# Layer norms on rows in place, by token halves, with the next stage's first two units going token by token

## The reference, cut to what matters

```python
# first block (one layer)
x = x + merged @ w_out
h = rmsnorm(x, g_mlp)
x = x + square(relu(h @ w_mlp_in)) @ w_mlp_out
h = rmsnorm(x, g_final)

# second block; post_norm(x, sub, g, b) = layer_norm(ALPHA * x + sub, g, b)
for layer in range(2):
    if layer == 1:
        shared = nsa_shared_kv(h, ...)          # six key/value slots, kv_w
    h = post_norm(h, 0.5 * swiglu(h, w1, w3, w2), ln_g[layer, 0], ln_b[layer, 0])
    mix = chunked_sgu_mixer(h, ...) if layer == 0 else nsa_mixer(h, shared, ...)
    h = post_norm(h, mix, ln_g[layer, 1], ln_b[layer, 1])
    h = post_norm(h, 0.5 * swiglu(h, w1, w3, w2), ln_g[layer, 2], ln_b[layer, 2])
return h
```

## Time and profile before

| what | us |
|---|---|
| median of 3 runs | 1635.03 |
| lowest, highest run | 1631.24, 1640.81 |
| span of the profiled execution | 1638.5 |
| TensorE busy in it | 1546.8 |
| VectorE, ScalarE, GpSimd busy | 928.9, 712.0, 152.5 |

### The profile page before, as it was taken

The page is one execution under the profiler, slowest core; times in us unless marked ns, Lnnn a source line. Parts: engine busy times, 40 slices in busy tenths (PEclk is TensorE's granted clock), DMA queues, the critical chain, the costliest instruction groups (busy, mean ns, idle before and its releaser), DMA issues.

```text
span 1638.5 us, 26119 instructions
## 1 busy us (share of the span) xinstructions
PE 1546.8 (94%) x10700; PEld 1395.6 (85%) x10700; DVE 928.9 (57%) x1372; ACT 712.0 (43%) x924; POOL 152.5 (9%) x85
## 2 busy tenths in 40 slices
PE   8878979999999999999999998999999899999997
PEld 6868877998889999898789997999998866689996
DVE  5835266655575555667765557544555373365556
ACT  5436534434344443653344444344433464344442
POOL 0124510000020000200120002000001300110001
PEclk9969999999999999999999999999999987999999
DMA  8853343655666555553455653675554510255561
GB/s 256 138 145 95 117 150 129 205 179 182 197 225 196 196 184 180 181 181 139 144 183 182 189 193 129 183 254 182 191 191 134 181 51 1 77 180 180 182 196 58
DMA packets 191020, 267.75 MB, mean 163 GB/s; under 512 B 5581, under 2 KB 164465, under 8 KB 190687
## 3 DMA queue, kind: packets, MB, share of 16 engines
q1 hardware_dynamic: 186192, 250.05, 47.0%
q0 software_dynamic: 3872, 15.39, 4.0%
q10 hardware_dynamic: 878, 1.21, 0.3%
HBM read 261.40 MB, written 4.19 MB: 162 GB/s over the span
## 4 chain that ended last, share of the span: by engine, by line
PE 85%; DVE 7%; ACT 5%; DMA 2%; issue 1%; SPq 0%; POOL 0%; DVEq 0%; ACTq 0%
PE bank L627 83%; DMA ring<-in_w_in 2%; DVE hT_lo L1633 1%; PE bank L650 1%; ACT act_out L1246 1%; ACT split L1228 1%; DVE split L1554 1%; DVE xn L1605 1%; ACT hT_hi L1254 1%; DVE act_out L1625 0%; DVE stats L1580 0%; DVE xn L1811 0%; ACT attend L1328 0%; ACT arena L1276 0%; DVE attend L1742 0%
## 5 line engine op out<-in xcount | busy, mean ns | idle before, releaser
L627 PE MATMUL bank<-hT_hi,split 128*128 128x256 f32 x4240 | 771.0, 282 | 22.7 <-DVE hT_lo L1633 17.1
L1554 DVE TENSOR_TENSOR split<-ring,split 128x2048 fp32r<-128x2048 f32 x218 | 496.9, 2284 | 440.6 <-ACT split L1228 440.5
L627 PEld LDWEIGHTS bank<-hT_hi,split 128*128 128x128 f32 x4240 | 658.2, 189 | 30.9 <-issue 25.0
L1228 ACT ACTIVATE split<-ring 128x2048 fp32r<-128x2048 f32 x232 | 440.7, 1905 | 412.3 <-PE bank L627 373.3
L627 PE MATMUL bank<-hT_lo,split 128*128 128x256 f32 (+1 forms) x2120 | 595.5, 281 | 0.0
L627 PEld LDWEIGHTS bank<-hT_lo,split 128*128 128x128 f32 (+1 forms) x2120 | 400.6, 189 | 2.5
L627 PE MATMUL bank<-split,hid_hi 128*128 128x512 f32 x1088 | 316.7, 396 | 0.0
L627 PEld LDWEIGHTS bank<-split,hid_hi 128*128 128x128 f32 x1088 | 200.1, 188 | 45.6 <-issue 0.6
L627 PE MATMUL bank<-split,hid_lo 128*128 128x512 f32 x544 | 178.7, 395 | 0.0
L627 PE MATMUL bank<-split,hT_hi 128*128 128x256 f32 (+1 forms) x672 | 134.8, 303 | 6.3 <-POOL hT_lo L2088 3.6
L2066 POOL TENSOR_TENSOR resid<-xn,gain_bc 128x1024 f32<-128x1024 f32 x12 | 30.7, 2558 | 1068.4 <-DVE xn L1605 853.5
(11 more groups left out here) (170 smaller groups left out, 979.6 us busy)
## 6 DMA issues: line engine op xcount, KB each, us to landing
ring<-in_ffn_w SPq DMA_DIRECT2D x132, 1024.0 KB, 5.2
ring<-in_w_in SPq DMA_DIRECT2D x19, 1024.0 KB, 5.4
ring<-in_w_mlp_in SPq DMA_DIRECT2D x16, 1024.0 KB, 5.4
ring<-in_w_mlp_out SPq DMA_DIRECT2D x16, 1024.0 KB, 5.0
ring<-in_sgu_w_in SPq DMA_DIRECT2D x16, 1024.0 KB, 5.5
ring<-in_sgu_w_out SPq DMA_DIRECT2D x8, 1024.0 KB, 4.9
ring<-in_kv_w SPq DMA_DIRECT2D x6, 1024.0 KB, 5.0
ring<-in_w_out SPq DMA_DIRECT2D x4, 1024.0 KB, 5.0
```

The lines of the kernel that those rows point to most:

```text
L627: ins = pe.matmul(o, lhsT, rhs, start=start, stop=stop)
L1228: act.activation(split_hi[:, split_slot(q), 0:n], ring[:, u % SLOTS, 0:n], ACT.Copy).then_inc(hi_ready, 1)
L1554: dve.tensor_tensor(split_lo[:, place, 0:n], ring[:, u % SLOTS, 0:n], split_hi[:, place, 0:n].bitcast(F32), ALU.subtract).then_inc(split_r ...
```

## The change

Norms 2 to 9 are rewritten, and the work around them is reordered:

- VectorE applies gain and bias to the rows in place, in halves of 512 columns (finish): rows minus mean times gain, then times the reciprocal deviation plus bias. GpSimd's residual step and the copy xn are gone (norm 2 still writes xn). TensorE transposes these rows; ScalarE rounds 512 columns straight out of the bank, VectorE makes the low part straight out of it.
- In down_last each bank of the first tokens has its own signal, and the first tokens' transposes stand before the last addition. The dummy products at norms 2 to 8 are gone.
- The last down unit of each stage is split into a fourth place (EXTRA, the buffer `two`). The next stage's first unit is split before the last hidden chunk, its second unit is rounded right after it and its low part is made by GpSimd (SECOND). The third is rounded by ScalarE inside the norm.
- Behind norms 3, 5 and 8 the first chunk's w1 and w3, behind norm 4 sv 0 and sv 1, behind norm 6 kv 3 and kv 5 go token by token: both units on the first tokens, then both on the second. The second tokens' transposes stand inside the second unit, before k = 4 and k = 6. A hidden chunk made that way is transposed on TensorE (turn_hidden).
- The kv units are taken in the order 3, 5, 0, 1, 2, 4. The turning of the gating weights (turn_ws) moves into feed-forward 0. The first turn of the feed-forward loops, and the last one on ScalarE and VectorE, are unrolled. Norm 9 writes the rows that SyncE stores in four pieces.

```diff
+KV_ORDER = (3, 5, 0, 1, 2, 4)
+TOK = {0: 3, 1: 5, 3: 8}
+EXTRA = SPLIT
+LAST = {("wout", 3), ("md", MLP_CHUNKS - 1), ("so", 7), ("wo", 3)} | {("w2", f, FFN_CHUNKS - 1) for f in range(N_FFN)}
+SECOND = {("mu", 1), ("w3", 0, 0), ("sv", 1), ("w3", 1, 0), ("kv", 5), ("q", 0), ("w3", 3, 0)}
...
+        elif name in LAST:
+            slots.append(EXTRA)
+        else:
+            slots.append(turn % SPLIT)
+            turn += 1
...
# TensorE, down_last
-                add(1, 0, 0)
+                add(1, 0, 0).then_inc(half_done, 1)
                 add(1, 0, 1).then_inc(half_done, 1)
                 add(0, 1, 0)
                 add(1, 1, 0).then_inc(half_done, 1)
                 add(0, 1, 1).then_inc(unit_used, 1)
+                if n < 9:
+                    for h in range(2):
+                        turn_rows(n, 0, h)
                 add(1, 1, 1).then_inc(unit_used, 1)
+            def turn_rows(n, b, h):
+                rows = xn if n == 2 else resid
+                pe.wait_ge(xn_ready, 4 * n + 2 * b + h + 1)
+                o = open_tile(("n", n, b, h))
+                for k in range(4):
+                    ins = turn(o[:, k * P:(k + 1) * P], rows[:, b, (h * 4 + k) * P:(h * 4 + k + 1) * P])
...
# TensorE, up_tok_split
                 for k in range(KT):
                     if norm is not None:
                         normed(norm, b, k)
+                    if turns is not None and k in (4, 6):
+                        turn_rows(turns, 1, (k - 4) // 2)
...
+                def first_by_tokens(n):
+                    have(("w1", f, 0))
+                    o = open_tile(("f", f, 0, 0))
+                    up_tok_split(o[:, 0:S], parts(("w1", f, 0), KT), UC, 0, n)
+                    have(("w3", f, 0))
+                    up_tok_split(o[:, S:2 * S], parts(("w3", f, 0), KT), UC, 0, turns=n).then_inc(tile_done, 1)
+                    o = open_tile(("f", f, 0, 1))
+                    up_tok_split(o[:, 0:S], parts(("w1", f, 0), KT), UC, 1, n)
+                    up_tok_split(o[:, S:2 * S], parts(("w3", f, 0), KT), UC, 1).then_inc(tile_done, 1)
...
+                    if c == 0 and f in TOK:
+                        turn_hidden()
...
# ScalarE
-            def norm(n):
-                deviation(n, 0)
-                turned(n, lambda: deviation(n, 1))
+            def norm(n, between, after=None):
+                load_table(ACT.Sqrt)
+                deviation(n, 0)
+                round_turned(n, 0)
+                if between:
+                    round_unit(between)
+                deviation(n, 1)
+                if after:
+                    after()
+                round_turned(n, 1)
...
# VectorE
-            def norm(n):
-                norm_rows(n)
-                norm_turned(n)
+            def add(n, b, h):
+                if b and h:
+                    dve.wait_ge(unit_used, UNITS[ACC_DONE[n]] + 1)
+                else:
+                    dve.wait_ge(half_done, 3 * (n - 2) + 2 * b + h + 1)
+                r = resid[:, b, h * 512:(h + 1) * 512]
+                link(dve.scalar_tensor_tensor(out=r, in0=r, scalar=ALPHA if n >= 4 else 1.0, in1=acc[2 * b + h][:, :],
+                                              op0=ALU.mult, op1=ALU.add))
+                link(dve.bn_stats(stats[:, b, h, :], r))
+            def finish(n, b):
+                ins = dve.bn_aggr(mv[:, b, :], stats[:, b, 0:2, :])
...
+                for h in range(2):
...
+                        link(dve.scalar_tensor_tensor(out=d, in0=r, scalar=mv[:, b, 0:1], in1=gain_bc[:, cols],
+                                                      op0=ALU.subtract, op1=ALU.mult))
+                    if h == 0:
+                        dve.wait_ge(sd_ready, NB * n + b + 1)
+                        link(dve.reciprocal(rstd[:, b:b + 1], sd[:, b:b + 1]))
...
+                        ins = dve.scalar_tensor_tensor(out=d, in0=d, scalar=rstd[:, b:b + 1], in1=bias_bc[:, cols],
+                                                       op0=ALU.mult, op1=ALU.add)
+                    ins.then_inc(xn_ready, 1)
+            def norm(n):
+                add(n, 0, 0)
+                add(n, 0, 1)
+                finish(n, 0)
+                add(n, 1, 0)
+                if n < 9:
+                    low_turned(n, 0)
+                add(n, 1, 1)
+                finish(n, 1)
+                if n < 9:
+                    low_turned(n, 1)
...
# GpSimd
-            residual(3)
+            low_unit(("mu", 1))
+            load_rows(3)
+            low_unit(("w3", 0, 0))
+            load_rows(4)
```

More of the change, by code:

```diff
@@ L335, in two_blocks @@
         at = [0]
+        qT = take(at, 8, S)
+        pc = take(at, NB, NH, 32)
+        pcT = take(at, NG, S)
         ka = take(at, 4, 2, S)
@@ L606, in _ @@
             ffn(1)
-            some("kv", 6)
+            for i in KV_ORDER:
+                load(("kv", i))
             some("cw", 4)
@@ L699, in down_split, with down_last, add @@
                 ins.then_inc(unit_used, 1)
-            def down_last(before, last):
+            def down_last(before, last, n):
                 units = [before]
-                def add(n, b, h):
-                    unit, act = units[n]
+                def add(u, b, h):
+                    unit, act = units[u]
                     for k in range(2):
@@ L1004, in ffn, with chunk @@
                 clear_acc()
                 done = MLP_CHUNKS + f * FFN_CHUNKS + (8 if f else 0)
-                def chunk(k, i):
+                def chunk(c):
+                    have(("w1", f, c + 1))
+                    tiles = [open_tile(("f", f, c + 1, ft)) for ft in range(2)]
+                    up_w1(tiles, parts(("w1", f, c + 1), KT))
+                    if c == 0 and f in TOK:
+                        turn_hidden()
+                    have(("w3", f, c + 1))
+                    up_w3(tiles, parts(("w3", f, c + 1), KT))
+                    have(("w2", f, c))
+                    pe.wait_ge(hid_ready, done + c + 1)
+                    return parts(("w2", f, c), 2), hidden_chunk(c % FFN_BODY)
@@ L1033, in last, with turn_ws, first_two, rest_of_norm @@
                     return parts(("w2", f, FFN_CHUNKS - 1), 2), hidden_chunk((FFN_CHUNKS - 1) % FFN_BODY)
-                down_last(before, last)
-            norm(2)
+                down_last(before, last, ACC_NORM[("w2", f, FFN_CHUNKS - 1)])
+            def turn_ws():
+                pe.wait_ge(ws_ready, 1)
+                for i in range(2):
+                    o = open_tile(("wst", i))
+                    for k in range(4):
+                        ins = turn(o[:, k * P:(k + 1) * P], ws[:, 4 * i + k, :])
+                        settle(ins)
+                    ins.then_inc(tile_done, 1)
+            def first_two(units, tiles, n):
+                for j in range(2):
+                    have(units[j])
+                    o = open_tile(tiles[j][0])
+                    up_tok_split(o[:, 0:S], parts(units[j], KT), S, 0, None if j else n,
+                                 turns=n if j else None).then_inc(tile_done, 1)
+                for j in range(2):
+                    o = open_tile(tiles[j][1])
+                    up_tok_split(o[:, 0:S], parts(units[j], KT), S, 1, None if j else n).then_inc(tile_done, 1)
+                    owed[0] += 1
+            def rest_of_norm(n):
+                for h in range(2):
+                    turn_rows(n, 1, h)
+            rest_of_norm(2)
             mlp(2)
-            norm(3)
-            ffn(0, 3)
-            norm(4)
-            for i in range(8):
+            ffn(0)
+            first_two([("sv", i) for i in range(2)], [[("sv", i, b) for b in range(NB)] for i in range(2)], 4)
+            for i in range(2, 8):
                 have(("sv", i))
@@ new lines, in gelu_v @@
+            def gelu_v(i, b):
+                o = tile_ready(act, ("sv", i, b))
+                act.activation(vtok[:, b, i * UC:(i + 1) * UC], o[:, 0:S], ACT.Gelu).then_inc(frees(("sv", i, b)), 1)
+            norm(4, mixer[2], lambda: gelu_v(0, 0))
+            gelu_v(1, 0)
+            gelu_v(0, 1)
+            round_unit(mixer[3])
+            gelu_v(1, 1)
+            round_unit(mixer[4])
+            for i in range(2, 8):
+                for b in range(NB):
+                    gelu_v(i, b)
+                round_unit(mixer[i + 3])
```

572 lines of the change are left out of this document (332 added, 240 removed).

## The result

The changed kernel takes 1595.44 us in the median (1590.98 to 1598.52, four runs) against 1636.20 for the kernel before with its runs of the same comparison (1631.24 to 1640.81, four runs): 40.8 us less between the medians, and a ratio of 0.9738, 95% interval 0.9708 to 0.9768, which is 38 to 48 us of 1636.20. The forecast was 1590.0 with 1583 to 1610. The profiled executions differ by 1638.5 - 1593.3 = 45.2 us; the sum was 45.0. The total agrees better than its parts: two stages are off by 5 to 6 us, with opposite signs, and some 5.5 us come from a thing that no term holds.

What follows compares the result with a forecast made beforehand. TensorE, busy 94% of the span, was taken to lose time only at eight norms; shorter norm chains, clock recovery and small costs summed to 45.0 us off the 1635.03 median: 1590.0 us, range 1583 to 1610.

Steps and rivals of the forecast that it cites:

- The chain of the new norm: From T0, VectorE's start on the first tokens' second-half addition, next stage's first product at about T0 + 6.95, formerly 16.1.
- The clock at norms 5, 6 and 8: TensorE no longer idles over a few tenths there, so half-clock losses of 2.75, 1.6 and 1.6 us come back.
- The rival that feared for it (1606): Clock falls without dummies at all seven norms: 16 us less gain, 1606 us; chance 0.09.
- GpSimd in VectorE's way: Rival: late GpSimd work blocks VectorE's gain step, 2.5 us at each of six norms, 1605 us; chance 0.10.
- Moved orders in kv: Key-value stage: two value units go first, the last units cover VectorE's compressed-key work; listed as costing nothing.
- 3.1 us for norm 7: Ahead of the attention stage, which needs all tokens: first product at about T0 + 13.0 instead of 16.1.
- Norm 2: No bias and cheaper scaling: 12.4 us against 13.4 before, a gain of 1.0.
- The clock loss that I had charged with 1.6: At norm 2, a new TensorE idle stretch from 6.7 to 11.0 was charged 1.6 us.
- Norm 9: At the end, VectorE's last bias at 10.8 us after T0 instead of 12.7: a gain of 1.9.
- Given back behind the norm: Rival: TensorE then waits for following units, all eight places returning all but 1 us; 1627 or more; chance 0.08.
- the slower case: Rival: hidden-chunk detour and peeled loops hurt 44 feed-forward chunks; at 1.2 us each, 1643 us; chance 0.05.
- The length of a chunk: Middle of a stage can give nothing: 256-column products every 0.117 us, 5.6 us a unit, TensorE always busy.

Runs made afterwards that it cites:

- pair_signal: Changed kernel, with VectorE's addition of the first tokens' first half made to wait for both halves' last down products: 1606.25 us, ratio 0.9795.
- before_no_dummies: Kernel before the change, without its dummy products at norms 2 to 9: 1643.24 us, ratio 1.0015.
- second_on_vector: Changed kernel, with the low parts of six of the seven second units moved from GpSimd to VectorE: 1600.08 us, ratio 0.9755.
- gpsimd_twice: Changed kernel, with GpSimd making the low part of each second unit twice: 1633.12 us, ratio 0.9940.
- kv_low_early: Changed kernel, with VectorE making unit kv 4's low part ahead of its wait for the swapped keys: 1590.17 us, ratio 0.9686.
- after_same: Changed kernel run again with no edit, the measure for the other experiments: 1590.23 us, ratio 0.9693.
- by_features: Changed kernel without the token order: the next stage's first two units take both tokens at once: 1624.23 us, ratio 0.9929.

## Why the prediction was right, and where it was wrong

**The chain of the new norm: right.** Forecast and measured at norm 6, from T0: gain step 1.69 and 1.78, the first tokens' rows ready at 3.3 and 4.8 against 3.51 and 4.96, first product 6.95 and 7.16. The 0.2 us lie mostly in the gain and bias steps, four of 0.75 where I had 0.72, the upper of the two bounds and still short. At norm 5 the first product comes at T0 + 8.16, 1.0 late (below). pair_signal shows that the chain on VectorE is what sets the norm: what is added to it comes out in the stage. The four stages behind norms 3, 4, 5 and 8, clock and turned chunks included, give 33.0 us against 31.0, but the three feed-forward stages among them owe some 1.2 us each to the shorter chunks; without that the four give 29.5 (the mixer's stage not corrected), and norm 5 lacks most of what is missing: 8.9 where 10.4 were forecast.

**The clock at norms 5, 6 and 8: right.** With gaps of 0.5 to 0.8 us on TensorE it stays at 1.00 behind norms 6 and 8 without dummies, and norm 5's products keep their full speed; two experiments show how near the edge that is (a gap of 1.25 at norm 5 and one of 0.88 at norm 8, with the clock down behind each). The rival that feared for it (1606) had the Trainium skill's view on its side, that the throttled state is the default which activity lifts (TensorE: Matmul & The Clock Gate, What's actually happening). before_no_dummies agrees at norms 2 and 3, where it pays 1.5 and 2.7 us for the dummies that did hold the clock. The changed kernel pays nothing at norm 3, where useful products stand in the gap, and pays at norm 2, where none do (see the small terms).

**GpSimd in VectorE's way: the mechanism is real, the place right, the margin was small.** The claim that GpSimd ends near T0 + 1.2, ahead of the gain step, held at norm 6 (T0 + 1.26) and failed at norm 5 (T0 + 2.98), where the rounding came later; that cost VectorE 1.0 us, and of it second_on_vector could win back nothing in the stage. gpsimd_twice shows what a late one costs, 3.5 to 6.9 us a norm: more than the rival's 2.5.

**"Moved orders in kv": wrong.** The sentence that failed is that the compressed-key work on VectorE then has the last units as cover. I named who covers that work, and didn't ask when its input would now come, nor who is queued behind it. Behind the 8.73 us wait stood kv 4's low part, and TensorE stood behind that: 4.0 us, and the clock after it. kv_low_early, which moves that one operation, gives 5.1 to 6.5 us where 6.0 were missed.

**The attention stage: luck, and it hid the miss.** I had 3.1 us for norm 7. Its first product comes at T0 + 13.6 instead of 16.1, so 2.5 are the change's. The other 5 go with a half-clock stretch that was shorter in the profiled execution of after than in that of before: behind the idle 3.5 us the granted clock is 0.50 for 23.9 us in before and for 13.7 in after. All ten profiled executions without the tail's dummies have the idle 3.5 us. Only after_same and by_features do the first pair of products behind it wholly at full clock, and theirs are the shortest stages, 153.2 and 153.0; the others of the changed norm 7 took 157 to 163, and gpsimd_twice 167.6 with a later norm; the two with dummies took 152 and 153. The kernel before has 165.0 in one execution and 160.8 in that without dummies, so the size of this excess is that of two single executions.

**The small terms.** Norm 2: 12.8 against 13.4 before, so 0.6 rather than 1.0. The clock loss that I had charged with 1.6 is there: the first product behind the norm, before and after, and a window of after:

```profile
277.82 0.36 PE L627 MATMUL bank<-hT_hi,split 128*128 128x256 f32 x1 [1.19 <-DVE hT_lo L1633]
...
278.25 0.55 PE L685 MATMUL bank<-hT_hi,split 128*128 128x256 f32 x1 [0.38 <-DVE hT_lo L1851]
```

```profile
278.00:281.00 3.00, 2.75 (x13) 2.78 (x14) 0.79 (x2) 0.50 (x1) 0.00 (x0) 0.50 0.48 175
```

Some 2.8 us of work at half clock lose 1.4. The stage's difference is 0.0 all the same, because the MLP's 16 shorter chunks give 0.8. Norm 9: 13.7 against 15.2, 1.5 rather than 1.9, again the 0.75 steps. "Given back behind the norm" and the slower case did not come: the stages are shorter by what their norms give, and by no less.

**The length of a chunk: held to be unchanged, and it wasn't.** The prediction read the pitch of a 256-column product as 0.117 from nine products in 1.06 us; that is 0.1178, and a unit takes 5.65 us before, not 5.6. It says that the middle of a stage can give nothing. It gave 0.11 us a chunk, an estimated 5.5 in all, from a cause that stays open.

By the total of the profiled executions the prediction looks exact to 0.2 us; by the medians it promised 45.0 and got 40.8. By its terms the new chain and the clock behind it came out within about 1.5 us at each norm, 6 us were missed in the key-value stage (7 with its shorter chunks taken off), and 5 from the attention stage's clock and 5.5 from shorter chunks were handed to it. That these nearly cancel against the misses, and against 1.0 us ahead of norm 2 that is chance, is luck. What decides, at the 3.5 us idle stretch, whether the clock falls stays open.

## What to carry to other kernels

When a stall can't be shortened further, order the work by the half of the data that is ready first: here the token order of two units was worth 31 of 37 us. When the producers of an in-order queue's wait are moved, write down when it will now end and what stands behind it, not only what covers it. Sum the profile by stages against the prediction's terms before believing a total, measure a stretch that the change should leave alone (here a hidden chunk), and repeat the profiled run: a stage whose length varies from one execution to the next gives a change credit that isn't its own.

## What the runs showed of the hardware

One idle stretch of 3.5 us on TensorE, ahead of batches with small products, is followed by a half-clock stretch of very different length: the attention stage took 153 to 163 us for the same work. With 13 dummy products of 0.23 us in the stretch, which leave 0.50 us of it idle, it took 152 to 153. In the kernel before, dummies that ended 3.4 us ahead of the next useful product (norms 5, 6 and 8) were followed by half clock and were worth 0.4 us or less; those that ended 1.19 and 2.41 us ahead of it (norms 2 and 3) were followed by full clock and were worth 1.5 and 2.7 us. So a dummy is worth its place by how close it comes to the next useful product; it needn't reach it.

The same stream of 256-column products, at a granted clock of 1.00 and without a gap, ran at 117.8 ns a product in the two kernels without the change and at 116.7 in the ten with it. What sets it isn't shown.

A VectorE operation on two SBUF operands took 4.68 us instead of 0.75 and ended 0.5 us behind a GpSimd operation that had begun 0.4 us before it. Two VectorE operations in a row, additions out of a bank with their statistics, kept 0.69 us beside the same GpSimd work.
